# Sums of squares in the dilated-attention rounds: one FP32 product replaced by two products of rounded operands

## What is computed

```python
qa = rms_norm_2(aq.reshape(B, S, ATTN_HEADS, ATTN_HEAD_DIM), q_norm_g[l])
ka = rms_norm_2(ak.reshape(B, S, ATTN_HEADS, ATTN_HEAD_DIM), k_norm_g[l])
y_att = dilated_attention_group(qa, ka, av.reshape(B, S, ATTN_HEADS, ATTN_HEAD_DIM))
```

## Time and profile before

| | |
|---|---|
| runs of the kernel, median (lowest to highest) | 1366.87 us (1366.6 to 1366.9) |
| the profiled execution, device time | 1367.36 us |
| its span, first to last instruction | 1365.7 us |
| PE busy | 1354.9 us, 99% of the span |
| DVE busy | 880.8 us, 64% |
| ACT busy | 589.2 us, 43% |
| the three full-length dilated rounds that hold the six sums | 868.9 to 944.6 us of the span |

### The profile page before, as it was taken

How to read it: one execution, slowest core, us unless ns; L and a number is a source line. 1 busy time by engine, 2 the same in 40 slices (tenths; PEclk the granted TensorE clock), 3 DMA queues, 4 the chain that set the end, 5 groups by cost and what they waited for, 6 DMA issues and landing times.

```text
span 1365.7 us, 19386 instructions
## 1 busy us (share of the span) xinstructions
PE 1354.9 (99%) x6846; PEld 1107.0 (81%) x6846; DVE 880.8 (64%) x1479; ACT 589.2 (43%) x984; POOL 57.5 (4%) x119
## 2 busy tenths in 40 slices
PE   9999999999999999999999999999999999999999
PEld 7877777778988888888887688777898888888887
DVE  6667676678787777774337978766576566564221
ACT  5455545554463233223223735666454444443221
POOL 0000000000002111210100000000000000000000
PEclk9999999999999999999999999999999999999999
DMA  5222212213316555555443112111212322323332
GB/s 209 93 78 78 77 63 78 78 63 126 102 62 208 192 194 190 188 196 162 138 139 113 47 63 78 62 62 62 78 59 99 102 92 93 105 94 116 89 96 88
DMA packets 43015, 147.08 MB, mean 108 GB/s; under 512 B 5584, under 2 KB 6096, under 8 KB 42960
## 3 DMA queue, kind: packets, MB, share of 16 engines
q1 hardware_dynamic: 34848, 120.37, 27.1%
q0 software_dynamic: 7824, 25.70, 5.6%
q10 hardware_dynamic: 288, 0.27, 0.1%
HBM read 143.69 MB, written 2.10 MB: 107 GB/s over the span
## 4 chain that ended last, share of the span: by engine, by line
PE 92%; DVE 5%; issue 1%; ACT 1%; DMA 1%; ACTq 0%; DVEq 0%; POOLq 0%
PE bank L665 61%; PE bank L860 14%; PE bank L683 4%; PE bank L799 3%; PE bank L886 2%; PE bank L907 2%; PE bank L979 2%; PE bank L925 1%; PE bank L1149 1%; DVE w_lo L1962 1%; PE bank L928 1%; PE bank L1270 0%; DMA raw<-in_w_mix 0%; DVE xT L2464 0%; DVE xT L2277 0%
## 5 line engine op out<-in xcount | busy, mean ns | idle before, releaser
L1962 DVE TENSOR_TENSOR w_lo<-raw,w_hi 128x1024 fp32r<-128x1024 f32 (+1 forms) x223 | 266.5, 1196 | 153.0 <-ACT w_hi L1346 151.9
L1346 ACT ACTIVATE w_hi<-raw 128x1024 fp32r<-128x1024 f32 (+1 forms) x223 | 230.6, 1035 | 287.2 <-PE bank L665 262.1
L665 PE MATMUL bank<-h_hi,w_hi 128*128 128x512 f32 x864 | 342.9, 397 | 2.7 <-DVE h_lo L2511 1.3
L665 PE MATMUL bank<-h_hi,w_lo 128*128 128x512 f32 x864 | 336.6, 390 | 0.0
L665 PE MATMUL bank<-h_lo,w_hi 128*128 128x512 f32 x864 | 336.5, 389 | 0.0
L665 PEld LDWEIGHTS bank<-h_hi,w_hi 128*128 128x128 f32 x864 | 162.1, 188 | 42.7 <-issue 3.7
L665 PEld LDWEIGHTS bank<-h_hi,w_lo 128*128 128x128 f32 x864 | 162.2, 188 | 34.2
L665 PEld LDWEIGHTS bank<-h_lo,w_hi 128*128 128x128 f32 x864 | 162.3, 188 | 33.6 <-issue 1.4
L665 PE MATMUL bank<-f_hi,w_lo 128*128 128x512 f32 x352 | 136.9, 389 | 0.0
L665 PE MATMUL bank<-f_hi,w_hi 128*128 128x512 f32 x352 | 136.9, 389 | 0.0
L665 PE MATMUL bank<-f_lo,w_hi 128*128 128x512 f32 x352 | 136.9, 389 | 0.0
(11 more groups left out here) (372 smaller groups left out, 1935.2 us busy)
## 6 DMA issues: line engine op xcount, KB each, us to landing
raw<-in_w_up SPq DMA_DIRECT2D x66, 512.0 KB, 3.2
ada<-in_w_ada POOLq DMA_DIRECT2D x96, 256.0 KB, 3.1
raw<-in_w_mix SPq DMA_DIRECT2D x47, 512.0 KB, 3.2
raw<-in_w_down SPq DMA_DIRECT2D x32, 512.0 KB, 3.5
raw<-in_w_in SPq DMA_DIRECT2D x24, 512.0 KB, 3.3
raw<-in_w_gate SPq DMA_DIRECT2D x22, 512.0 KB, 3.2
raw<-in_w_out SPq DMA_DIRECT2D x16, 512.0 KB, 3.3
raw<-in_w_down SPq DMA_DIRECT2D x16, 384.0 KB, 3.3
```

The costliest lines, as they stand in the source:

```text
L665: last = pe.matmul(to[:, :], wt[:, slot, k, :], act_[:, rhs0 + k, :], start=(k == first and n == 0), stop=(k == K - 1 and n == 2))
L1346: act.activation(w_hi[:, s, k0:K, :], raw[:, s, k0:K, :], ACT.Copy).then_inc(hi_ready[s], 1)
L1962: dve.tensor_tensor(w_lo[:, s, k0:K, :], raw[:, s, k0:K, :], w_hi[:, s, k0:K, :].bitcast(F32), ALU.subtract).then_inc(split_ready[s], 1)
```

## The change

In rounds 8 to 10 the squares are split like every other operand. ACT squares the bank a second time, into the rounded `qk_hi`, for queries and for keys (one buffer for both), between the first square and the copy. DVE subtracts (`square_rest`): `qk_lo` is `qk_sq` less `qk_hi`, and signals `sq_split`. PE multiplies `blk`, now stored in the rounded type, with `qk_hi` and with `qk_lo`, both summed in the same bank, in the place of one FP32 product with `qk_sq`. The sums for the first pair stay one FP32 product of the same values.

On DVE the remainder of the queries stands ahead of `split_lo(0)`, that of the keys ahead of both `dilated_distances`. On PE the query sum moves from step 11 to step 13, the key sum from step 19 to step 20 (in round 8 it stood at 20 already).

```diff
-DILATED_TURNS = {24: (4, 9, 11, 15, 19, 20), 21: (3, 8, 8, 13, 13, 18)}
+DILATED_TURNS = {24: (4, 9, 13, 15, 20, 20), 21: (3, 8, 8, 13, 13, 18)}
...
-        blk = sb("blk", [P])
+        blk = sb("blk", [P], F32R)
...
                 pe.wait_ge((q_staged, k_staged)[m], p + 1)
                 pe.wait_ge(qk_rs[0], p + 1) if m else pe.wait_ge(vd_ready, p)
-                pe.matmul(O1[:, :], blk[:, :], qk_sq[:, m, :], start=True, stop=True).then_inc(qk_ms, 1)
+                pe.wait_ge(sq_split, 2 * p + m)
+                pe.matmul(O1[:, :], blk[:, :], qk_hi[:, :], start=True, stop=False)
+                pe.matmul(O1[:, :], blk[:, :], qk_lo[:, m, :], start=False, stop=True).then_inc(qk_ms, 1)
...
-                norm_k += 1 if i == 8 else 0
...
                 then(act.activation(qk_sq[:, 0, :], dilated_bank(p, 0)[:, :], ACT.Square))
+                if p:
+                    then(act.activation(qk_hi[:, :], dilated_bank(p, 0)[:, :], ACT.Square))
                 act.activation(next_q[:, :], dilated_bank(p, 0)[:, :], ACT.Copy).then_inc(q_staged, 1)
...
                 then(act.activation(qk_sq[:, 1, :], dilated_bank(p, 1)[:, :], ACT.Square))
+                if p:
+                    then(act.activation(qk_hi[:, :], dilated_bank(p, 1)[:, :], ACT.Square))
                 act.activation(next_k[:, :], dilated_bank(p, 1)[:, :], ACT.Copy).then_inc(k_staged, 1)
...
+            def square_rest(p, m):
+
+                dve.wait_ge((q_staged, k_staged)[m], p + 1)
+                dve.tensor_tensor(qk_lo[:, m, :], qk_sq[:, m, :], qk_hi[:, :].bitcast(F32), ALU.subtract).then_inc(sq_split, 1)
+
...
                 store_turned(i, 0)
                 if i < 11:
+                    square_rest(p + 1, 0)
                     split_lo(0)
...
                 store_turned(i, 1)
                 if i < 11:
+                    square_rest(p + 1, 1)
                     dilated_distances(p + 1, 0)
                     dilated_distances(p + 1, 1)
                     split_lo(1)
```

More of the change, by code:

```diff
@@ L302, in build @@
         (qk_sq,), qk_end = region(gla_end, ("qk_sq", [2, S], F32))
+        (qk_lo,), _ = region(gla_end, ("qk_lo", [2, S], F32R))
+        (_, _, qk_hi), _ = region(tmp_at, ("hbuf_too", [2, S], F32), ("sq_first", [S], F32), ("qk_hi", [S], F32R))
         (_, _, qk_r), _ = region(tmp_at, ("hbuf_at", [2, S], F32), ("sq_at", [2, S], F32), ("qk_r", [2, S], F32))
@@ L367, in build @@
         first_half_hi, first_half_lo = signal("first_half_hi"), signal("first_half_lo")
-        first_sq, first_sum = signal("first_sq"), signal("first_sum")
+        first_sq, sq_split = signal("first_sq"), signal("sq_split")
         first_half_in, first_x_in = signal("first_half_in", 16), signal("first_x_in", 16)
@@ L523, in _ @@
                                     base=0, pattern=[[-1, P]], channel_multiplier=1))
-            for t, v in ((blk, 0.0), (eps6, NORM_EPS), (eps5, SUBLN_EPS)):
+            then(pool.memset(blk[:, :].bitcast(F32), 0.0))
+            for t, v in ((eps6, NORM_EPS), (eps5, SUBLN_EPS)):
                 then(pool.memset(t[:, :], v))
-            then(pool.memset(blk[0:64, 0:64], 1.0))
-            then(pool.memset(blk[64:128, 64:128], 1.0))
+            then(pool.memset(blk[0:64, 0:64].bitcast(F32), 1.0))
+            then(pool.memset(blk[64:128, 64:128].bitcast(F32), 1.0))
             pool.drain().then_inc(const_ready, 1)
@@ L768, in qk_norm_sums @@
                 pe.wait_ge(qk_rs[0], 1) if m else None
-                pe.matmul(S1[:, :], blk[:, :], qk_sq[:, m, :], start=True, stop=True).then_inc(qk_ms, 1)
+                pe.matmul(S1[:, :], blk[:, :].bitcast(F32), qk_sq[:, m, :], start=True, stop=True).then_inc(qk_ms, 1)
             def first_values(banks):
@@ L820, in _ @@
             pe.wait_ge(const_ready, w.next(const_ready))
-            pe.wait_ge(first_sum, 1)
+            pe.wait_ge(sq_split, 1)
             pe.matmul(T1[:, :], ones[:, :], sqacc[:, :], start=True, stop=True).then_inc(ms_ready, 1)
@@ L2030, in _ @@
             then(dve.tensor_tensor(gate_b[:, 0:2, :], gate_b[:, 0:2, :], gate_b[:, 2:4, :], ALU.add))
-            dve.tensor_tensor(sqacc[:, :], gate_b[:, 0, :], gate_b[:, 1, :], ALU.add).then_inc(first_sum, 1)
+            dve.tensor_tensor(sqacc[:, :], gate_b[:, 0, :], gate_b[:, 1, :], ALU.add).then_inc(sq_split, 1)
             dve.wait_ge(lam_in, w.next(lam_in, times=2))
```

## The result

| | before | changed |
|---|---|---|
| runs, median (lowest to highest) | 1366.9 us (1366.6 to 1367.33) | 1373.62 us (1372.88 to 1375.31) |
| the profiled execution | 1367.36 us | 1372.88 us |
| its span | 1365.7 us | 1371.2 us |

The ratio is 1.0048 with an interval of 1.0036 to 1.0059: slower by 6.7 us, outside the predicted range of 1368.8 to 1372.4. The direction was right, the sum of 4.05 us too small.

The account below looks back on a forecast made before the run. PE, busy for 99% of the span, was taken to set the pace. Later scores after rounds 8 to 10, 2.09 + 0.98 + 0.98 = 4.05 us, against the 1366.87 us median gave 1370.9 us, range 1368.8 to 1372.4 (8 in 10).

Parts of the forecast that it names:

- What PE gains: On PE, two rounded products take 0.46 us in place of 0.86 in four sums; 2.6 us saved over all six.
- What ACT and DVE get: Two 0.62 us squares per round on ACT and two subtractions on DVE; the distances and what follows start 2.75 us late.
- First place, the key sum: PE waits at the key sum for DVE's subtraction: 2.6 us in round 8, 1.2 us in round 9.
- Second place, the scores: The next round's scores wait for the normalised keys and start 2.09 us later after round 8, 0.98 after 9 and 10.
- the fourth rival: Something else is late besides, such as the last store of turned probabilities against the next values product: 1373 us; chance 0.06.
- The third rival, the clock: PE's clock falls to 1.2 GHz after round 8's wait: up to 3.7 us more, 1374.6 us; chance 0.06.
- The sum: The later scores of the three rounds added up: 2.09 + 0.98 + 0.98 = 4.05 us, giving 1370.9 us.

Follow-up runs that it names:

- e4: The changed kernel with only the queries' squares split, the keys' sum again one FP32 product; 1366.87 us, ratio 0.9998.
- e1: The changed kernel with the last store of turned probabilities put ahead of the normalised keys on DVE in rounds 8 to 10; 1373.29 us, ratio 1.0040.
- e5: The changed kernel with only the keys' squares split, the queries' sum again one FP32 product; 1371.33 us, ratio 1.0030.
- e2: The changed kernel with the key sum on PE at step 22 in place of 20, behind the last transposes; 1376.1 us, ratio 1.0064.
- e3: The changed kernel with the keys' subtraction on DVE between the two distance operations in place of ahead of both; 1370.04 us, ratio 1.0022.
- e9: The changed kernel with unused products (9 in round 8, 4 in rounds 9 and 10) filling PE's key-sum wait; 1373.09 us, ratio 1.0049.
- e6: The changed kernel, keys' subtraction between the distances, store and normalised keys ahead of the slot-1 remainder, last transposes and key sum at step 22; 1366.38 us, ratio 0.9994.
- e12: The changed kernel once more, unaltered, beside the same runs of the kernel before as e9; 1373.79 us, ratio 1.0049.

## Why the prediction was off

- **What PE gains: right.** Two products hold PE for 0.48 us (from 910.03 to 910.51, the query sum of round 9) where 0.46 was taken, and e4 found the 0.40 of a query sum in rounds 9 and 10.
- **What ACT and DVE get: right.** 0.63 us for each square, both arriving in `k_staged`, the subtraction where it was predicted to 0.01 us, the distances 2.74 us late. Of the bounds for a square (0.50 and 0.62) the row with the wait behind it was the right one, and the Trainium skill's overlap of 93 ns (ScalarE: Activation LUTs, "What ACT_TABLE_LOAD costs") doesn't show between these squares, as the prediction had taken it. That it is stated for instructions without a wait between them is the prediction's reading: the Trainium skill says only "back-to-back" there. The row of 0.60 us with 0.50 to the next start agrees with that reading.
- **First place, the key sum: right.** Predicted 2.6 and 1.2 us, measured 2.20 and 1.11; the start times agree to 0.01. The profile counts the idle time from the end of PE's last product, the prediction from 0.23 us after its start. Counted its way the waits are 2.36 and 1.27, so in round 8 PE also arrived 0.2 us later than predicted.
- **Second place, the scores: this step failed.** The prediction said "Second the next round's scores, which need the normalised keys" and gave them 1.93 us in hand, 0.82 in round 8, so it expected a wait of about 0.5 us where 1.08 was measured. The scores also need the last store of turned probabilities, which stands 0.66 us behind the keys on DVE, and their slack was 1.12 and 0.00. With these in the same sum: 2.75 + 1.63 + 1.63 = 6.0 in the place of 4.05. e1 showed the pair's end to be what counts, e5 confirmed the slack at another delay. The store was named under the fourth rival, but only against the values product that reads its result, where it has time; the scores, which overwrite the bank that it reads, were overlooked. That rival's 1373 lies near the measured time by luck: the wait that it priced did not come.
- **The third rival, the clock, came in part.** It fell after the wait in round 8, as that rival said, and cost 0.42 us, not 3.7: it lasted some 3 us, and most of that lay beside the wait for DVE. The rule named there (the Trainium skill, TensorE: Matmul & The Clock Gate, "Why this matters for your kernels") is for longer idle gaps than 2.20 us and does not, as the prediction had it, speak against every wait. These traces agree with it for the 3.30 us of e2. They also show the clock at 0.50 behind 2.20 and 2.24 us, where the Trainium skill's rule gives no warning, and at 1.00 behind 2.25, 2.36 and 2.37.
- **The sum** then is 6.0 + 0.4 = 6.4 against 6.5 measured in the rounds and 6.7 in the medians. The range was too narrow because its ends moved only durations, and neither stood for a second signal in the same wait.

What stays open: e3 had a wait of 2.25 us at the same place and kept a whole clock in its profiled execution, and e2 kept it behind two waits of 2.36 and 2.37 us. So the length of the wait alone does not decide, and no run here says what does. That filling the wait keeps the clock rests on one trace (e9) and on the counts above. Whether rounds 9 and 10 could give the whole 0.8 us wasn't tried beyond e6.

## What to carry to other kernels

Before an operation is put ahead of others on a queue, look up every semaphore that its waiting reader waits for, and take the slack from the last of the signals; two of them from one engine look like one in a profile, and the gap between the named releaser's end and the start is what tells them apart (0.81 us here, against 0.10 to 0.21 where the named one is real). An engine that is busy 65% of the time can still have no slack at one place, so an operation that waits belongs behind work that does not. And what a cheaper operation on the engine that sets the pace brings depends first on where its extra work stands in the other engines' queues: the same work gave +6.5 us in the rounds in one order and -0.9 in another (e6).

## What the runs showed of the hardware

- The clock of PE fell to half behind an idle stretch of 2.20 us (changed), 2.24 (e12, and e1) and 3.30 us (e2), for some 3 us each time, while PE was at work again; in e1 the fall came some 1.2 us after PE had started again, in the changed kernel 0.2 us before it did. It stayed whole behind 2.25 us in e3, behind 2.36 and 2.37 us in e2 and behind the waits of about 1.1 us in rounds 9 and 10.
- What such a fall costs depends on what lies beside it: 0.42 us where PE had to wait for DVE soon after, 1.7 us where it met the scores that DVE starts from.
- PE starts 0.10 to 0.21 us after the end of the DVE operation that releases it: 0.10 behind the keys (e1), 0.15 behind the subtraction, 0.21 behind the store.
